# Two transformer blocks in one program: a scan's work moved between engines, the second mixer's closing stages merged with its projections, and the second experts' first nine weight pieces loaded one stage earlier

## The chip, the cores and the metric

The program runs on one core of one Trainium2 chip. The core has TensorE (PE, matrix products; its weight loads are a row of their own, PEld), VectorE (DVE), ScalarE (ACT), GpSimd (POOL) and SyncE (SP, which here only issues transfers), each with its own instruction stream, joined by semaphores. The metric is the device time of one execution in microseconds.

## The reference, cut to what matters

Two blocks run one after the other on 512 tokens of width 1024, all in float32. The first has a token mixer with neighbourhood attention and a two-way state-space scan (SSD), then 16 experts. The second has a mixer of two branches, then 32 small experts. Three places matter here.

The scan, chunk by chunk (128 tokens), for 4 groups of 8 heads and in both directions:

```python
    x = (xs * dt[..., None]).reshape(Bsz, nc, SSD_CHUNK, SSD_GROUPS, R, P)
    states = jnp.einsum('bclgn,bcgrl,bclgrp->bcgrpn', Bc, decay_to_end, x)
    def step(h, inp):
        dec, st = inp
        return dec[..., None, None] * h + st, h
    ...
    y_diag = jnp.einsum('bcgls,bcgrls,bcsgrp->bclgrp', cb, Lm, x)
    y_off = jnp.einsum('bclgn,bcgrpn,bcgrl->bclgrp', Cc, jnp.moveaxis(h_prev, 0, 1), jnp.exp(a_cs))
```

It runs first over the context (256 tokens, only the states count), then over the 512 tokens (states and y). The state after the last chunk of each direction is not used by anything.

The second mixer: `merged = gate_rw * (y_rw @ w_branch_rw) + gate_mla * (y_mla @ w_branch_mla)`. y_rw is a recurrent mix that ends in a normalisation by head, a scale and shift, a bonus and a gate. y_mla is an attention whose queries and keys come from a projection down (672 columns), two root-mean-square norms, a rotation by position, and projections up.

The second experts (`hier_moe`): each token goes to 2 of 32 experts, `(silu(gt) * up) @ w_down[e]`, with gt and up from a 1024x512 matrix of the expert.

## The kernel before, in words

Work is cut into stages. A stage is a function that holds one instruction stream for each engine (`@block.tensor`, `@block.vector` and so on), and between two stages all engines meet at a barrier. Inside a stream the order is the order of the code, and semaphores say who waits for whom.

`ssd_scan` walks 48 units (direction, chunk, group): 16 of the context, then 32 of the main tokens, of which the first 16 write y for the first time and the last 16 add to it. For each unit POOL makes `xd` and `xde` (inputs times step size, times decay) and, for main units, `seg_in` (L1277, 128x1024). PE makes the new state's part `st` (L1313), the product with the old state `yo` (L1318), the next unit's `seg` and `cb` (L1300, L1302, one PSUM buffer each) and `yd` (L1323). ACT takes exp of `seg` into `lx`. DVE masks `cb` into `cbm` (L1345), multiplies `lx` by it (L1349), decays the state (L1358), adds `st` (L1359), and makes y (L1362 to L1371). A helper `Steps` (its objects are called `link`) makes an engine wait for its own last result.

The second mixer ends in this chain of stages, all at barriers: `rw_states` (the recurrence), `rw_finish` (norm, scale, bonus and gate of y_rw, on DVE), a transposition of y (`rw_y_t`), the branch product (`rw_br`), the load of a block of constants, the projection down (`p_mla`), `mla_rows` (norms and rotation tables), two transpositions (`mla_qn_t`, `mla_kvn_t`), `mla_up`, and `causal_attention`. Weights for the next projection are asked for by SP while the last one runs (`WeightsAhead`, two buffers).

The second experts: `route_experts` (stage `hm_choose`) scores and ranks tokens. `fine_experts` (stage `hm`) then runs in a loop whose count is read from the device; in this trace it goes round once. It takes the experts in 16 pairs. For a pair, two 2 MB pieces (gate and up, `gu`) and one 2 MB piece (`down`) are needed. Three pieces are loaded in the choice stage (`hm_kept`), the other 45 go through a ring of five slots that SP starts to fill when `hm` begins:

```python
            for n in range(len(ring.order)):
                if n >= HM_SLOTS:
                    kind, u, _ = ring.order[n - HM_SLOTS]
                    sp.wait_ge({"gu": gu_done, "down": down_done}[kind], u + 1)
                ring.load(sp, n)
```

POOL gathers the tokens of each pair by index from DRAM (L3462, `xrow`), PE turns them (L3487), DVE scales them (L3582), PE multiplies by the weights (L3501), and so on.

## Time and profile before

| what | value |
|---|---|
| runs before | 3734.84, 3745.22, 3734.08 us, median 3734.84 us |
| the profiled execution | 3730.5 us, of which the span of the trace is 3728.7 us |
| PE busy | 3155.3 us, 85% of the span |
| DVE, ACT, POOL busy | 1146.8, 478.1, 320.3 us |
| mean granted TensorE clock | 0.925 of full speed |
| moved by DMA | 669.34 MB |

The profiled execution is one run, 4.3 us below the median of the three that were timed. Busy times are sums of instruction durations. The ends of matrix products are modelled, and a product can show as busy while the next one has started. A bracket behind a row gives the idle time of that engine before the row and, after the arrow, what ended it.

### The profile page before, as it was taken

How to read it: one execution, taken by the hardware profiler on the slowest of the kernel's cores; microseconds unless marked ns; L12 is line 12 of the kernel's file. 1: busy time of each engine (PE TensorE's matmuls, PEld its weight loads, DVE VectorE, ACT ScalarE, POOL GpSimd, SP SyncE). 2: the span in 40 equal slices, each digit the busy share in tenths (PEclk: the TensorE clock that was granted, in tenths of full speed). 3: DMA queues.
4: the chain of work that ended last, by engine and by line, in shares of the span. 5: the costliest groups of instructions: out<-in, count | busy, mean ns of one | idle time of the engine just before them, and what ended most of it. 6: DMA issues, size and time to landing. Idle time of an engine off the chain costs nothing. (4 is left out here: it accounts for less than half of the span.)

```text
span 3728.7 us, 38059 instructions
## 1 busy us (share of the span) xinstructions
PE 3155.3 (85%) x15800; PEld 1675.7 (45%) x15800; DVE 1146.8 (31%) x2119; ACT 478.1 (13%) x898; POOL 320.3 (9%) x261
## 2 busy tenths in 40 slices
PE   6997799996989999598999999987967577995974
PEld 4444545562654444444434443434447443534331
DVE  2234602554893200401011101113264613512112
ACT  1002500111112100100000000001123101301111
POOL 0003000003972000000000000000012100000000
PEclk9998998996999999699999999998989788995997
DMA  6621021100001221399999999995100120015996
GB/s 255 248 68 46 1 71 46 46 23 1 23 1 68 90 68 45 159 410 418 423 416 423 415 428 424 423 388 179 34 1 3 52 76 24 23 45 215 398 425 277
DMA packets 130497, 669.34 MB, mean 180 GB/s; under 512 B 15994, under 2 KB 44061, under 8 KB 97305
## 3 DMA queue, kind: packets, MB, share of 16 engines
q1 hardware_dynamic: 115385, 630.24, 42.1%
q10 hardware_dynamic: 11488, 28.31, 2.0%
q0 software_dynamic: 3456, 8.39, 0.6%
q8 instruction: 125, 2.05, 0.2%
q14 instruction: 43, 0.35, 0.0%
HBM read 653.28 MB, written 14.69 MB: 179 GB/s over the span
## 5 line engine op out<-in xcount | busy, mean ns | idle before, releaser
L1907 PE MATMUL ec_wide<-ec_ring,ec_xg 128*64 128x512 f32 x2048 | 457.9, 601 | 24.3 <-issue 18.6
L1907 PEld LDWEIGHTS ec_wide<-ec_ring,ec_xg 128*64 128x64 f32 x2048 | 148.2, 138 | 313.9 <-issue 309.7
L1941 PE MATMUL ec_acc<-ec_ring,ec_hidT 128*64 128x512 f32 x1024 | 232.8, 608 | 38.4 <-DMA ec_ring<-in_w_exp_down 36.3
L2066 DVE TENSOR_SCALAR ec_xg<-ec_piece,ordered 128x128 f32<-128x128 f32 x64 | 21.9, 404 | 583.0 <-PE ec_piece L1955 583.0
L1941 PEld LDWEIGHTS ec_acc<-ec_ring,ec_hidT 128*64 128x64 f32 x1024 | 84.5, 140 | 184.6 <-issue 184.6
L3501 PE MATMUL hm_gu<-hm_ring,hm_xg 128*64 128x512 f32 x480 | 110.8, 615 | 23.7 <-DMA hm_ring<-in_moe_w_gu 22.3
L1955 PE MATMUL ec_piece<-ec_sel,x 128*128 128x128 f32 x512 | 124.4, 405 | 3.3 <-DVE ec_sel L2048 3.3
L1955 PEld LDWEIGHTS ec_piece<-ec_sel,x 128*128 128x128 f32 x512 | 122.9, 336 | 9.1 <-issue 5.7
L2631 POOL TENSOR_TENSOR solve_T<-const_rw,solve_T 128x512 f32<-128x512 f32 x8 | 10.1, 1266 | 1330.2 <-DVE solve_T L2669 1330.2
L1107 PE MATMUL conv_main<-hT,conv_early 128*128 128x512 f32 x192 | 85.3, 599 | 1.6 <-DVE bcT L1183 1.6
L526 PE MATMUL p_rkv_acc<-ahead_rkv,h2mT 128*128 128x384 f32 x256 | 84.5, 494 | 2.3 <-DVEq L534 2.3
L1107 PE MATMUL conv_main<-hT,conv_late 128*128 128x512 f32 x192 | 85.8, 600 | 0.0
L2030 ACT ACTIVATE ec_hidT<-ec_acc 128x512 f32<-128x512 f32 x32 | 17.4, 594 | 519.3 <-PE ec_acc L1930 519.3
L3501 PEld LDWEIGHTS hm_gu<-hm_ring,hm_xg 128*64 128x64 f32 x480 | 39.2, 141 | 94.3 <-issue 92.5
L1277 POOL TENSOR_TENSOR ssd_seg_in<-const_all,a 128x1024 f32<-128x1024 f32 x32 | 77.3, 2416 | 0.6 <-PE ssd_cb L1302 0.6
L2081 DVE TENSOR_TENSOR branch<-branch,ec_piece 128x512 f32<-128x512 f32 x64 | 44.0, 687 | 107.2 <-PE ec_piece L1973 107.2
L1973 PE MATMUL ec_piece<-ec_y,ec_selT 128*128 128x512 f32 x128 | 63.8, 622 | 7.3 <-DVE ec_selT L2075 6.1
L1286 POOL TENSOR_TENSOR ssd_xde<-ssd_xd,dec 128x512 f32<-128x512 f32 x48 | 68.7, 1431 | 3.8
L1300 PE MATMUL ssd_seg<-ssd_seg_in,const_all 128*128 128x512 f32 x128 | 62.4, 610 | 4.7 <-DVE ssd_cbm L1345 4.7
L526 PEld LDWEIGHTS p_rkv_acc<-ahead_rkv,h2mT 128*128 128x128 f32 x256 | 49.4, 193 | 37.0 <-DVEq L534 2.5
L2676 DVE TENSOR_TENSOR solve_T<-solve_T,solve_wide 64x512 f32<-64x512 f32 (+1 forms) x80 | 50.5, 632 | 50.0 <-PE solve_wide L2562 42.0
L1358 DVE TENSOR_TENSOR ssd_state<-ssd_state,dec 128x512 f32<-128x512 f32 x40 | 59.7, 1492 | 18.4 <-PE ssd_st L1313 18.4
(620 smaller groups left out, 5016.5 us busy)
## 6 DMA issues: line engine op xcount, KB each, us to landing
ec_ring<-in_w_exp_gate SPq DMA_DIRECT2D x64, 2048.0 KB, 14.0
ec_ring<-in_w_exp_up SPq DMA_DIRECT2D x64, 2048.0 KB, 22.2
ec_ring<-in_w_exp_down SPq DMA_DIRECT2D x64, 2048.0 KB, 17.7
hm_ring<-in_moe_w_gu SPq DMA_DIRECT2D x30, 2048.0 KB, 18.8
hm_ring<-in_moe_w_down SPq DMA_DIRECT2D x15, 2048.0 KB, 15.9
ahead_qkv<-in_w_in SPq DMA_DIRECT2D x10, 2048.0 KB, 9.6
key<-in_w_ada ACTq DMA_DIRECT2D x4, 2048.0 KB
v<-in_w_ada ACTq DMA_DIRECT2D x4, 2048.0 KB, 10.2
```

The costliest lines, as they stand in the source:

```text
L526: last = pe.matmul(acc[0:rows, bank, 0:cols], stat(j), mov(j), start=(j == 0), stop=(j == kt - 1))
L1107: last = pe.matmul(main[:, i % 2, :], w[:, j, m * P:(m + 1) * P], hT[:, j, :], start=(j == 0), stop=(j == KD - 1))
L1277: pool.tensor_tensor(seg_in[:, m % 2], cum.unsqueeze(1).to_broadcast([P, HG, P]), spread(a[:, tile(u), hs:hs + HG], P), ALU.mult).then_inc ...
L1286: pool.tensor_tensor(xde[:, n % 2].rearrange("p (h e) -> p h e", h=HG), xd[:, n % 2].rearrange("p (h e) -> p h e", h=HG), spread(e2, 64), ...
L1300: pe.matmul(seg[:, h, :], k.const("after" if d == 0 else "before"), seg_in[:, m % 2, 4 * h:4 * h + 4].rearrange("p h l -> p (h l)"), start ...
L1358: link(dve.tensor_tensor(sv, sv, spread(e3, 64), ALU.mult))
L1907: last = pe.matmul(wide[half(e), b, :], xg[:, u % 2, j, half(e)], w[e][:, a, b * 512:(b + 1) * 512], start=(j == 0), stop=(j == KD - 1))
L1941: last = pe.matmul(acc[half(e), h, :], hidT[:, f, half(e)], w[e][:, r, h * 512:(h + 1) * 512], start=(f == 0), stop=(f == FT - 1))
L1955: last = pe.matmul(piece[:, m % 2, i * P:(i + 1) * P], x[:, t, HALF * h + i::KD], sel[:, t, :], start=(t == 0), stop=(t == LT - 1))
L1973: pe.matmul(piece[:, m % 2, :], selT[:, t * P:(t + 1) * P], y[:, h * 512:(h + 1) * 512], start=True, stop=True).then_inc(piece_done, 1)
L2676: dve.tensor_tensor(x, x, wide[s][half(c), c, first * 256:512], ALU.subtract).then_inc(T_done[s], 1)
L3501: last = pe.matmul(gu[half(e), u % 2, :], xg[:, u % 2, j, half(e)], w[e][:, j, :], start=(j == 0), stop=(j == KD - 1))
```

## The change

Three parts, in one edit.

**Scan.** `seg_in` is made by ACT (8 copies of 128x128 with a scale each) in place of one POOL instruction. The decay of the state goes from DVE to POOL. POOL prepares unit n+1 before it decays the state for unit n. The last 8 units make no `xde`, no `st` and no new state.

```diff
+            def decayed(n):
+                main, d, c, g = units[n]
+                if main:
+                    pool.wait_ge(off_ready, mains.index(n) + 1)
+                pool.wait_ge(state_done, n - chain + 1)
...
+                pool.tensor_tensor(sv, sv, spread(e3, 64), ALU.mult).then_inc(state_decayed, 1)
+
+            inputs(0)
+            for n in range(len(units)):
+                if n + 1 < len(units):
+                    inputs(n + 1)
+                if chain <= n < kept:
+                    decayed(n)
...
+            def segment_inputs(m):
+                main, d, c, g = units[mains[m]]
+                if m >= 2:
+                    act.wait_ge(seg_ready, m - 1)
+                cum = k.const("upto" if d == 0 else "from")
+                for h in range(HG):
+                    col = d * SSD_H + g * HG + h
+                    ins = act.activation(seg_in[:, m % 2, h, :], cum, ACT.Copy, scale=a[:, tile(units[mains[m]]), col:col + 1])
+                ins.then_inc(seg_built, 1)
...
-                    link(dve.tensor_tensor(sv, sv, spread(e3, 64), ALU.mult))
+                elif n < kept:
+                    dve.wait_ge(state_decayed, n - chain + 1)
                     dve.tensor_tensor(state[:, d, g, :], state[:, d, g, :], st[:, :], ALU.add).then_inc(state_done, 1)
```

POOL in `ssd_scan`, some main units of before:

```order
L1277 TENSOR_TENSOR ssd_seg_in<-const_all,a 128x1024
L1283 TENSOR_TENSOR ssd_xd<-xs,dt 128x512
L1286 TENSOR_TENSOR ssd_xde<-ssd_xd,dec 128x512
L1277 TENSOR_TENSOR ssd_seg_in<-const_all,a 128x1024
L1283 TENSOR_TENSOR ssd_xd<-xs,dt 128x512
L1286 TENSOR_TENSOR ssd_xde<-ssd_xd,dec 128x512
```

and of the changed kernel:

```order
L1297 TENSOR_TENSOR ssd_state<-ssd_state,dec 128x512
L1279 TENSOR_TENSOR ssd_xd<-xs,dt 128x512
L1286 TENSOR_TENSOR ssd_xde<-ssd_xd,dec 128x512
L1297 TENSOR_TENSOR ssd_state<-ssd_state,dec 128x512
L1279 TENSOR_TENSOR ssd_xd<-xs,dt 128x512
L1286 TENSOR_TENSOR ssd_xde<-ssd_xd,dec 128x512
```

The 128x1024 instruction is gone from POOL and a 128x512 one on the state stands in its place.

**Second mixer.** `rw_finish_and_down` runs the finish of y_rw on DVE and, in the same stage, the projection down on PE, with ACT copying its results. Its weights lie in a tile that is free by then (`T4`) and are loaded by SP during `rw_states`, as are the rows of the norm, the positions, the constants and the residual. `rw_branch_and_rows` holds the transposition of y, the branch product, the rows of the attention and the transpositions of its norms in one stage. The weights of the branch are loaded there, at its start, and with them those of `mla_up`. After `mla_up` and after the attention a clearing of semaphores with a barrier is added.

```diff
+        @block.tensor
+        def _(pe):
+            for i, (c, t) in enumerate(tiles):
+                if t == 0:
+                    pe.wait_ge(down_loaded[c], 16)
+                if i >= 4:
+                    pe.wait_ge(product_taken, i - 3)
+                for j in range(KD):
+                    last = pe.matmul(acc[:, i % 4, 0:width], hT[:, j, t * P:(t + 1) * P], down_w[:, c, j * width:(j + 1) * width], start=(j == 0), stop=(j == KD - 1))
+                last.then_inc(product_ready, 1)
...
         @block.sync
         def _(sp):
...
+            for b in range(2):
+                ahead.load_first(sp, b, k.dram["w_branch_rw_2"][0], NY, 512)
+            for (dst, src), up_loaded in up_moves:
+                sp.dma_start(dst, src).then_inc(up_loaded, 16)
+            for b in range(2):
+                sp.wait_ge(product_ready, 4 * (b + 1))
+                ahead.load_first(sp, b, *w_next)
...
+            for j in range(NY):
+                turn(j, lambda t: y[:, t, j * P:(j + 1) * P], P).then_inc(y_flipped, 1)
+            pe.wait_ge(y_taken, NY)
+            for m in range(3):
+                product(m)
             pe.wait_ge(table_ready, 2)
             for i in range(3):
...
+                turn(i, lambda t: table[:, i, t, :], MLA_QK).then_inc(flipped, 1)
+            product(3)
+            for i, (dst, scale, j) in enumerate(columns):
...
+                turn(3 + i, lambda t: source[:, t, j * P:(j + 1) * P], P).then_inc(flipped, 1)
+                if i in (1, 3):
+                    product(4 + i // 2)
+            product(6)
+            product(7)
```

PE from the end of the recurrence to `mla_up`, before (the number behind x counts products of one kind in a row; `rw_br_b` is the branch, `p_mla` the projection down):

```order
L2717 MATMUL states_out<-states_S,rw_GT 64x64 x56
L402 MATMUL rw_y_t_pt<-const_all,rw_y 128x128 x16
L526 MATMUL rw_br_b_acc<-rw_yT,ahead 128x512 x32
L526 MATMUL p_mla_acc<-ahead,h2mT 128x336 x64
L2902 MATMUL mla_rows_bank<-const_all,mla_rows_table 96x128 x12
L402 MATMUL mla_qn_t_pt<-const_all,mla_qn 128x128 x12
L402 MATMUL mla_kvn_t_pt<-const_all,mla_kvn 128x128 x8
L2946 MATMUL mla_up_pq<-mla_qnT,mla_up_wq 96x512 x3
```

and of the changed kernel (`rw_fin_acc` is the projection down, `mla_rows_acc` the branch, `mla_rows_flip` the transpositions):

```order
L2772 MATMUL states_out<-rw_K,rw_GT 64x64 x56
L2851 MATMUL rw_fin_acc<-rw_T,h2mT 128x336 x64
L3000 MATMUL mla_rows_flip<-const_all,rw_y 128x128 x16
L3010 MATMUL mla_rows_acc<-mla_o,ahead 128x512 x12
L3000 MATMUL mla_rows_flip<-const_all,mla_v 96x128 x12
L3010 MATMUL mla_rows_acc<-mla_o,ahead 128x512 x4
L3000 MATMUL mla_rows_flip<-const_all,mla_gate 128x128 x8
L3010 MATMUL mla_rows_acc<-mla_o,ahead 128x512 x4
L3000 MATMUL mla_rows_flip<-const_all,mla_gate 128x128 x8
L3010 MATMUL mla_rows_acc<-mla_o,ahead 128x512 x4
L3000 MATMUL mla_rows_flip<-const_all,mla_gate 128x128 x4
L3010 MATMUL mla_rows_acc<-mla_o,ahead 128x512 x8
```

The number of products is the same. The projection down now comes first, and the transpositions of the attention's rows stand between products of the branch.

**Second experts.** The ring has nine slots and holds all 48 pieces. Its first nine are loaded in the choice stage (three early, six behind the store of the normalised rows). Since a later round of the loop needs them again, POOL reloads them by index inside the loop. In the first round every index lies out of range, so that no row is fetched; PE still waits for these transfers' semaphores. DVE sets the indices (2 small instructions at the end of the choice and of each round).

```diff
-HM_SLOTS = 5
-HM_KEPT = (("gu", 0, 0), ("gu", 0, 1), ("down", 0, 0))
+HM_SLOTS = 9
...
+    def load_again(self, pool, n):
+        kind, u, e = self.order[n]
+        pool.wait_ge(self.first_loaded[n], 16)
...
+            pool.indirect_dma_start(place, None, rows, bass.IndirectOffsetOnAxis(ap=self.rows[:, expert:expert + 1], axis=0),
+                                    bounds_check=HM_E * P - 1, oob_is_err=False).then_inc(self.again[n], 16)
...
+        if n < HM_SLOTS:
+            pe.wait_ge(self.first_loaded[n], 16)
+            pe.wait_ge(self.again[n], 16 if job[0] == "gu" else 32)
...
+                if u in (1, 2):
+                    for n in range(5 * (u - 1), min(5 * u, HM_SLOTS)):
+                        ring.load_again(pool, n)
```

POOL in `hm`, before (DMA is an indexed transfer that POOL issues):

```order
L3456 MEMSET hm_xrow 128x2048
L3462 DMA hm_xrow<-hm_xn_rows,hm_index 128x1024 x16
L3469 DMA hm_ring<-hm_y_rows,hm_source 128x1024 x8
```

and of the changed kernel:

```order
L3591 MEMSET hm_xrow 128x2048
L3597 DMA hm_xrow<-hm_xn_rows,hm_index 128x1024 x2
L1874 DMA hm_ring<-in_moe_w_gu,hm_again_rows 128x4096 x4
L1874 DMA hm_ring<-in_moe_w_down,hm_again_rows 128x2048 x2
L3597 DMA hm_xrow<-hm_xn_rows,hm_index 128x1024
L1874 DMA hm_ring<-in_moe_w_gu,hm_again_rows 128x4096 x2
L1874 DMA hm_ring<-in_moe_w_down,hm_again_rows 128x2048 x2
L1874 DMA hm_ring<-in_moe_w_gu,hm_again_rows 128x4096
L3597 DMA hm_xrow<-hm_xn_rows,hm_index 128x1024 x13
L3607 DMA hm_ring<-hm_y_rows,hm_source 128x1024 x8
```

Eleven indexed transfers are new on POOL's queue: six behind the second gather of tokens, five behind the third.

## Rows read from the trace of the kernel before

**Rows 1.** Windows of five stretches: us, length, busy per engine, PEclk, DMA share, GB/s

```profile
877.00:940.00 63.00, 35.47 (x37) 9.57 (x38) 23.53 (x24) 1.28 (x1) 43.78 (x38) 0.50 0.10 34
940.00:1027.30 87.30, 87.30 (x420) 56.69 (x418) 77.07 (x95) 17.40 (x17) 80.49 (x46) 1.00 0.00 1
1027.30:1135.00 107.70, 91.74 (x412) 55.21 (x410) 102.39 (x113) 15.35 (x15) 70.54 (x45) 1.00 0.00 1
2957.00:3100.00 143.00, 75.79 (x240) 45.99 (x240) 50.48 (x78) 8.27 (x23) 8.54 (x12) 0.79 0.28 99
3449.00:3690.00 241.00, 200.17 (x952) 86.14 (x952) 34.21 (x68) 28.19 (x47) 12.85 (x13) 0.96 0.95 395
```

**Rows 2.** Timeline of the scan's context units: start us, us, engine, line

```profile
887.36 0.69 DVE L1354 COPY ssd_state<-ssd_st 128x512 f32<-128x512 f32 x1 [2.30 <-PE ssd_st L1313]
...
907.73 2.05 PE L1313 MATMUL ssd_st<-ssd_xde,bc_rows 128*128 128x512 f32 x2 [2.54 <-DVE ssd_state L1359]
...
912.32 2.04 PE L1313 MATMUL ssd_st<-ssd_xde,bc_rows 128*128 128x512 f32 x2 [2.54 <-DVE ssd_state L1359]
```

**Rows 3.** Timeline of one of the last 16 main units

```profile
1046.44 1.08 PE L1313 MATMUL ssd_st<-ssd_xde,b_rows 128*128 128x512 f32 x2
...
1046.75 1.04 POOL L1283 TENSOR_TENSOR ssd_xd<-xs,dt 128x512 f32<-128x512 f32 x1 [3.28 <-PE ssd_yd L1323]
...
1047.43 0.91 DVE L1371 TENSOR_TENSOR y<-y,ssd_off 128x512 f32<-128x512 f32 x1
1047.87 1.37 POOL L1286 TENSOR_TENSOR ssd_xde<-ssd_xd,dec 128x512 f32<-128x512 f32 x1
...
1048.57 1.75 DVE L1349 TENSOR_TENSOR ssd_lx<-ssd_lx,ssd_cbm 128x1024 f32<-128x1024 f32 x1
1048.69 1.95 PE L1300 MATMUL ssd_seg<-ssd_seg_in,const_all 128*128 128x512 f32 x4 [0.31 <-DVE ssd_cbm L1345]
...
1050.70 1.90 PE L1323 MATMUL ssd_yd<-ssd_xd,ssd_lx 128*128 128x64 f32 x16
```

**Rows 4.** Groups by line and form, ACT at 128x128: busy us, mean ns

```profile
L661 ACT ACTIVATE hT_tiled<-open_xf,mod,scales 128x128 f32<-128x128 f32 x8 | 3.7, 457 | 17.8 <-DVE hT L721 17.7
...
L3070 ACT ACTIVATE mla_pT<-mla_flip 128x128 f32<-128x128 f32 x8 | 2.0, 256 | 0.0
```

**Rows 5.** Timeline from the finish of y to the projections up

```profile
2959.05 2.29 DVE L2797 TENSOR_REDUCE rw_fin_mean<-rw_y 128x32 f32<-128x2048 f32 x1 [1.65 <-PEq L3247]
...
2981.11 2.29 DVE L2812 TENSOR_TENSOR rw_y<-rw_y,rw_g 128x2048 f32<-128x2048 f32 x1
...
2991.76 25.48 PE L526 MATMUL rw_br_b_acc<-rw_yT,ahead 128*128 128x512 f32 x59
...
3025.34 37.94 PE L526 MATMUL p_mla_acc<-ahead,h2mT 128*128 128x336 f32 x128 [8.10 <-DVEq L534]
...
3100.02 4.55 PE L2946 MATMUL mla_up_pq<-mla_qnT,mla_up_wq 128*96 128x512 f32 x6 [10.94 <-DMA mla_up_wkv<-in_mla_w_kv_up]
```

**Rows 6.** DMA issues: KB each, median us from issue to landing

```profile
ahead<-in_w_branch_rw SPq DMA_DIRECT2D x1, 1024.0 KB, 7.3
```

**Rows 7.** Timeline of stage hm, POOL and PE

```profile
3408.89 1.20 POOL L3462 DMA_INDIRECT hm_xrow<-hm_xn_rows,hm_index  x1 [2.14 <-DVE hm_index L3576]
...
3419.97 1.97 PE L3487 MATMUL hm_flip<-const_all,hm_xrow 128*128 128x128 f32 x8 [10.06 <-DMA hm_xrow<-hm_xn_rows,hm_index]
...
3423.26 9.33 PE L3501 MATMUL hm_gu<-hm_kept,hm_xg 128*64 128x512 f32 x32 [1.32 <-DVE hm_xg L3582]
...
3457.58 7.03 PE L3501 MATMUL hm_gu<-hm_ring,hm_xg 128*64 128x512 f32 x32
...
3502.14 7.09 PE L3501 MATMUL hm_gu<-hm_ring,hm_xg 128*64 128x512 f32 x32 [0.44 <-DMA hm_ring<-in_moe_w_gu]
...
3669.71 8.78 PE L3501 MATMUL hm_gu<-hm_ring,hm_xg 128*64 128x512 f32 x32 [4.31 <-DMA hm_ring<-in_moe_w_gu]
...
3694.55 0.95 POOL L3469 DMA_INDIRECT hm_ring<-hm_y_rows,hm_source  x1 [0.30 <-issue]
```

**Rows 8.** DMA issues, the third gather of tokens alone: us to landing

```profile
hm_xrow<-hm_xn_rows,hm_index POOLq DMA_INDIRECT x1, 3.9
```

321 lines of the change are left out of this document (192 added, 129 removed).

## The prediction, as it was put on record

> **What bounds the kernel now.** I read the windows first, since the busy share of the whole run mixes stages with different limits. In the scan's first stretch of 63 us TensorE is busy for only 35.47 us, at half clock; in the next, 16 main units, it is busy for all of 87.30 us, so PE is the limit there; in the last 16 it has 91.74 of 107.7 us and DVE has 102.39, so something other than PE sets the pace [rows 1]. The timeline says what: single units and the bracket in front of each product [rows 2, 3]. For the second mixer, the window 2957 to 3100 shows PE busy for half and DMA at 0.28: a chain of short stages, limited by waiting in turn [rows 1, 5]. For the second experts the window gives a DMA share of 0.95 at 395 GB/s with PE at 200 of 241 us: nearly balanced, DMA slightly in the lead [rows 1], which the brackets confirm, 0.44 us of wait at the sixth pair and 4.31 at the last [rows 7].
>
> **Scan.** Context units first. The first eight have no decay: period 0.69+2.30=2.99 us. The last eight take 912.32-907.73=4.59, with PE waiting 2.54 for DVE's addition [rows 2]. There DVE does decay and addition between two `st`. With the decay on POOL, DVE and PE are back at about 2.99, and POOL has `xd`, `xde` and the decay, three 128x512 operations at 1.04 alone [rows 3], with gaps about 3.3. So 8 x (4.59-3.3) = 10 us saved. The bounds: none if POOL's three are each 1.4 long, as `xde` beside DVE is (1.37, [rows 3]), which makes 4.4; 13 at 2.99.
>
> The first 16 main units are 87.3/16=5.46 us each with PE always busy [rows 1]; no edit removes PE work, so they stay. DVE (77.07/16=4.8) and POOL (80.49/16=5.0) lose work there. ACT gains 8 copies of 128x128 per unit: 17.40/16=1.1 [rows 1] plus 8 x 0.26 to 8 x 0.46 [rows 4] is 3.1 to 4.8, under 5.46; this edit is hidden by PE and costs nothing unless a copy takes over 0.54 us.
>
> The last 16 main units take 107.7/16=6.73. From `st` to `seg` there are 1048.69-1046.44=2.25 us, since `seg` waits for `cbm`, which stands on DVE behind the addition to y [rows 3]; that order stays. From `seg` to `yd` are 1050.70-1048.69=2.01, and `yd` takes up to 1.90 (its modelled end overlaps the next product, about 1.75 until then) [rows 3]. A closed cycle of 6.0 to 6.16 remains, above PE's 5.46; decay of the state, and POOL's long `seg_in`, which fill the rest to 6.73, are gone. 16 x (0.57 to 0.73) = 9 to 12; I take 11.5. The dropped work of the last 8 units changes little of it, since the cycle contains `st` only as a start, and PE's end is not the limit; at most its 1.08 x 8=8.6 us more.
>
> The two engines disturb each other: `y+=` takes 0.91 and ends at 1048.34, while `xd` ended at 1047.79; `xde` takes 1.37 against the 1.04 of `xd`; the multiplication of `lx` takes 1.75 and starts while `xde` runs [rows 3]. The Trainium skill, "SBUF — State Buffer", section "SBUF: two separate sides", says that DVE with two SBUF inputs and GpSimd share a port pair that is an exclusive lock for the whole instruction. Taken at its word it would speak against moving decay from DVE to POOL: it buys nothing in an operation that both are blocked by. Read so, the lock is held in a unit for three POOL operations and two to three of DVE, by the rows 3x1.04+1.75+0.91=5.8 at the most, just below the cycle of 6.0; the trace agrees that they lengthen each other, but not that it binds. Were it to bind in the first 16 too, that is the third rival below.
>
> Scan: -10-11.5, so **-22** (bounds -8 and -30).
>
> **Second mixer.** The recurrence ends on DVE at 2959.05-1.65=2957.40, and `mla_up` starts at 3100.02 [rows 5]: 142.6 us. The changed chain, from the same start: a gap of 1.65 as now, the projection down of 37.94 [rows 5], at 2959.05 to 2997.0. DVE's finish lies beside it: 2983.40-2959.05=24.35 [rows 5], 13.6 shorter, so free; if the copies of ACT held it up by a few us it would still be. Its weights are asked for a stage earlier (`T4`), in `rw_states`. One copy more (0.5) and a barrier (1.65) give 2999.1. Now the branch stage: its weights are only asked for at its start, 7.3 us to landing for one 1 MB piece [rows 6]; 16 transpositions of y and their copies lie under that. So products begin at 3006.4. 64 of them at 25.48/59 make 27.6 [rows 5]; 32 transpositions of 128 columns at a quarter of a product's 0.43 are 3.5 between them. 3037.5; a merge of one or two DVE operations 0.8, the next stage's gap 1.65 and the added clearing of semaphores about 1: `mla_up` at 3041. The wait of 10.94 for its weights [rows 5] is gone, since they are asked for with the branch's, some 40 us earlier. 3100.02-3041 = **-59**. What left: loading of constants between stages (3025.34-2991.76-27.6 is 6 us), the norms and turns after the projection, which ran alone (3100.02-3025.34-37.94=36.7 with the wait), and DVE's finish alone. The price of the load at the stage's start is the largest unknown: nothing if it lay under the turns entirely, 7.3 as taken, and twice that if y's two pieces and `mla_up`'s come one behind another (14.6). The norms run on DVE and ACT during the products; they lay within 36.7-10.94=25.8 before, at most 28 are there now, so 8 us more at most if a chain of them ends behind the products. Bounds: -45 and -64. A wait of over 7 us on PE may also start it at half clock, which I put in this same bound.
>
> **Second experts.** Gather by POOL at 3408.89; PE turned its rows at 3419.97, 11.1 us on, 10.06 of them waiting for DMA [rows 7], because SP's ring pieces fill the queues. Alone, a gather lands in 3.9 [rows 8]. After the change the ring is full before, so 3412.8, then 3423.26-3419.97=3.3 to the first `gu`: 3416.1. But PE now also waits for the empty transfers; these come behind the second gather on POOL: from 3411.9, two at about 1.25 (rows: 0.95 to 1.20), landing 3.9 more, 3418.3. I take 3417.5, -6. The third pair stood 34.3 us after the first (3457.58-3423.26) [rows 7], so 3451.8. Then the step per pair while weights were ahead is (3502.14-0.44-3457.58)/3=14.71 [rows 7]; 13 steps give 3643.0 for the last pair. Whether DMA allows that: before, ten pairs at DMA's pace took (3669.71-3502.14)/10=16.76, for three pieces 5.59 each [rows 7]. Refill starts when the first `gu` is done (3417.5+9.33=3426.8) and the last pair's needs 37 pieces more: 3426.8+206.8+5=3638.6, in balance with 3643, so PE is the limit now, barely. 3669.71-3643 = 26.7, less 0.8 for DVE's index instructions: **-26**. Bounds: -12 if the empty transfers' cost scales with rows and bytes (2 MB against 0.5 MB, 4 x 0.95=3.8 us each, the first pair waiting for two of them and the third behind nine) and PE's step is 15.8 by lost clock; -31 at a step of 14.1.
>
> The price of an empty indexed transfer is in no row; the nearest are the full gathers (0.95 to 1.20 us on POOL, 3.9 to landing, [rows 7, 8]), and an empty one may cost more on POOL, if making the list of rows is what takes time, or less. The Trainium skill, "DMA: Bandwidth & Descriptors", section "Anatomy of one DMA — SWDGE (gpsimd) path", gives 2.0 us plus bytes over 436 GB/s; for the 0.5 MB gather an estimate of 3.2, against the row's 3.9, and 2.0 for an empty one. By it the gate on the first pair would lie before 3416.1+1 and the term would be -27.
>
> **Sum.** -22-59-26 = -107. On the profiled execution, 3730.5 (span 3728.7 and 1.8 around it), 3623.5; that run is 4.3 below the median of 3734.84, on which the same sum gives 3627.8. I forecast 3626. A measurement of this kernel tells about 0.3%, 11 us, from no change.
>
> **Rivals.**
> 1. Experts: the indexed reloads or lost clock eat half of the third term (-12): 3640. For it: eleven new transfers on POOL, on PE's path. Against: only the first three pairs see them. 0.15.
> 2. Mixer: the branch stage pays for its loads in turn and its norms end last (-45): 3640. For it: 7.3 us in [rows 6] and 4 MB behind one another. Against: 28 us of products cover most. 0.1.
> 3. Scan: the state's chain now goes PE, DVE, POOL, and a state needed by `yo` arrives late; 24 units then go at 5.9 and not 5.46, +11, so -10 in all: 3638. For it: PE has no slack in [rows 1]; against: POOL makes the inputs of the next unit ahead of the decay, so only a decay of 1.04 stands in the chain. 0.1. This is what the lock would do if it bound; the rule is the one that I cite above from the Trainium skill, "SBUF — State Buffer".
> 4. Slower in all. Making a list of rows on POOL takes not 1 us but time in proportion to rows times bytes, at a rate that no row bounds. Before the third pair's gather stand nine pieces' worth; below 34.3+12 us (5 us each) it is hidden. Over that all of PE waits: at t us a piece the loss is 9t-46, which beats 107+11 from t=18. For it: no row of an indexed 2 MB transfer; against: the 0.95 to 1.20 of the 0.5 MB one. 0.03. No change within 11 us needs this same case at t between 17 and 19, or the lower bounds of all three parts (-8, -45, -12) with a new wait of 54 us; for both together 0.02.
>
> The forecast itself, 3610 to 3642 by its bounds, has 0.6. For 8 in 10 the range takes in rivals 1 to 3 together with small shortfalls: 3606 to 3660. Faster 0.95, same 0.02, slower 0.03.
>
> **What would show it.** Context period 3.3 us and not 4.59; first main units still 5.46, last 6.0; ACT's copies under 0.5. One block of products of 38 us from about 2959 with DVE's finish beside it, a wait of near 7 before the branch, `mla_up` near 3041 less the scan's gain. First `gu` 6 us earlier relative to its gather, step 14.7 to the end, no DMA bracket over 1 before the last pairs. I am wrong if the first 16 main units lengthen, if PE waits for POOL's indexed transfers in later pairs, or if PE's step in the ring grows past 15.5.

## The result, and the profile after

The changed kernel runs in 3633.11 us (median of 4, 3625.31 to 3636.84) against 3736.16 us for the kernel before (median of 4); the ratio is 0.9717, 95% interval 0.9694 to 0.974. That is 103 us less. The forecast was 3626, with 3606 to 3660 as its range, so the median lies 7 us above it. The profiled execution is the slowest of the four, 3636.84 us, and its span is 3634.9, so the two profiled executions are only 93.8 us apart. The rest of this section says where.

The windows of the changed kernel, for the first and the last 16 main units, the second mixer's middle and the second experts (columns as in [rows 1]):

```profile
937.40:1024.70 87.30, 87.30 (x419) 56.63 (x417) 56.76 (x79) 55.13 (x147) 62.56 (x46) 1.00 0.00 1
1024.70:1119.80 95.10, 82.97 (x397) 52.12 (x395) 66.04 (x88) 47.54 (x126) 39.90 (x30) 0.99 0.00 1
2947.50:3029.50 82.00, 73.26 (x240) 43.24 (x241) 42.58 (x66) 14.15 (x35) 4.05 (x5) 0.94 0.23 81
3375.00:3590.00 215.00, 190.57 (x931) 79.78 (x930) 33.15 (x65) 25.83 (x43) 12.85 (x13) 0.97 0.98 410
```

Against [rows 1]: the first 16 main units take the same 87.3 us with PE always busy, and DVE has fallen from 77.07 to 56.76 us and ACT risen from 17.40 to 55.13 in them. The last 16 take 95 and not 108. In the mixer PE does the same work in 82 us and not 143. In the experts DMA's share rose from 0.95 to 0.98.

The timeline of the changed kernel, context units 10 and 11 and one of the last 16 main units:

```profile
916.48 2.04 PE L1329 MATMUL ssd_st<-ssd_xde,bc_rows 128*128 128x512 f32 x2 [1.08 <-DVE ssd_state L1390]
919.61 2.04 PE L1329 MATMUL ssd_st<-ssd_xde,bc_rows 128*128 128x512 f32 x2 [1.09 <-DVE ssd_state L1390]
...
1030.26 1.10 PE L1329 MATMUL ssd_st<-ssd_xde,b_rows 128*128 128x512 f32 x2
...
1031.46 0.69 DVE L1402 TENSOR_TENSOR y<-y,ssd_off 128x512 f32<-128x512 f32 x1
1031.65 1.41 POOL L1286 TENSOR_TENSOR ssd_xde<-ssd_xd,dec 128x512 f32<-128x512 f32 x1
1032.39 1.75 DVE L1381 TENSOR_TENSOR ssd_lx<-ssd_lx,ssd_cbm 128x1024 f32<-128x1024 f32 x1
1032.51 1.95 PE L1315 MATMUL ssd_seg<-ssd_seg_in,const_all 128*128 128x512 f32 x4 [0.29 <-DVE ssd_cbm L1377]
1033.02 2.02 POOL L1297 TENSOR_TENSOR ssd_state<-ssd_state,dec 128x512 f32<-128x512 f32 x1
1034.52 1.90 PE L1341 MATMUL ssd_yd<-ssd_xd,ssd_lx 128*128 128x64 f32 x16
1035.64 2.43 ACT L1355 ACTIVATE ssd_seg_in<-const_all,a 128x128 f32<-128x128 f32 x8
1036.25 1.08 PE L1329 MATMUL ssd_st<-ssd_xde,b_rows 128*128 128x512 f32 x2
```

The context step is 919.61-916.48=3.13 us where it was 4.59 [rows 2], and the main step is 1036.25-1030.26=5.99 where units of 6.7 and 7.05 took turns before. `seg` still waits 0.29 us for `cbm`, as in [rows 3]. ACT's 8 copies take 2.43 us, 0.30 each.

PE in the mixer of the changed kernel, from the recurrence's end to the projections up:

```profile
2949.30 36.40 PE L2851 MATMUL rw_fin_acc<-rw_T,h2mT 128*128 128x336 f32 x128 [1.83 <-PEq L209]
2987.82 2.96 PE L3000 MATMUL mla_rows_flip<-const_all,rw_y 128*128 128x128 f32 x16 [2.12 <-PEq L3395]
2993.37 13.23 PE L3010 MATMUL mla_rows_acc<-mla_o,ahead 128*128 128x512 f32 x24 [2.60 <-DMA ahead<-in_w_branch_rw]
...
3029.51 4.48 PE L3070 MATMUL mla_up_pq<-mla_qnT,mla_wq 128*96 128x512 f32 x6 [2.23 <-PEq L209]
```

Only 2.60 us of waiting for a transfer is left, and nothing of the 10.94 of [rows 5]. DVE in the same stage:

```profile
2965.25 0.35 DVE L2874 RECIPROCAL rw_fin_var<-rw_fin_var 128x32 f32<-128x32 f32 x1 [4.55 <-ACT rw_fin_var L2861]
...
2975.52 2.29 DVE L2882 TENSOR_TENSOR rw_y<-rw_y,rw_g 128x2048 f32<-128x2048 f32 x1
```

The finish waits 4.55 us for the square root, which stands behind ACT's third copy, and still ends at 2977.8, 8 us ahead of PE.

The experts' stage of the changed kernel, POOL and PE:

```profile
3342.37 1.20 POOL L3597 DMA_INDIRECT hm_xrow<-hm_xn_rows,hm_index  x1 [2.14 <-DVE hm_index L3710]
...
3345.69 0.99 POOL L1874 DMA_INDIRECT hm_ring<-in_moe_w_gu,hm_again_rows  x1 [0.30 <-issue]
3346.98 1.97 PE L3625 MATMUL hm_flip<-const_all,hm_xrow 128*128 128x128 f32 x8 [3.59 <-DMA hm_xrow<-hm_xn_rows,hm_index]
...
3350.27 8.82 PE L3637 MATMUL hm_gu<-hm_ring,hm_xg 128*64 128x512 f32 x32 [1.32 <-DVE hm_xg L3716]
...
3379.86 7.04 PE L3637 MATMUL hm_gu<-hm_ring,hm_xg 128*64 128x512 f32 x32
...
3525.89 7.04 PE L3637 MATMUL hm_gu<-hm_ring,hm_xg 128*64 128x512 f32 x32
3543.20 7.09 PE L3637 MATMUL hm_gu<-hm_ring,hm_xg 128*64 128x512 f32 x32 [3.04 <-DMA hm_ring<-in_moe_w_gu]
3559.67 7.09 PE L3637 MATMUL hm_gu<-hm_ring,hm_xg 128*64 128x512 f32 x32 [2.17 <-DMA hm_ring<-in_moe_w_gu]
3575.95 8.62 PE L3637 MATMUL hm_gu<-hm_ring,hm_xg 128*64 128x512 f32 x32 [4.28 <-DMA hm_ring<-in_moe_w_gu]
```

The first gate product comes 7.9 us behind its gather's start, where it came 14.4 behind it [rows 7]. Between the third and the thirteenth pair a step is (3525.89-3379.86)/10=14.60 us, and no wait for DMA shows before the fourteenth.

To compare stages I took the first start of one tile's products and the first start (or last end) of the next one's from the timelines of all the kernels run. The kernels scan_only, mixer_only and ring_only have one part of the change each and are explained below. "List" in the last two lines is PE's first product for the list of tokens (`hm_list`), which stands ahead of the first gather. Lengths in us:

| stretch | before | changed | scan_only | mixer_only | ring_only |
|---|---|---|---|---|---|
| convolution to first state product | 290.1 | 295.7 | 290.1 | 290.5 | 290.1 |
| scan | 254.2 | 233.6 | 233.5 | 254.4 | 254.2 |
| first experts | 957.0 | 961.1 | 961.8 | 967.1 | 958.6 |
| recurrence's end to projections up | 143.4 | 82.0 | 146.1 | 81.7 | 143.8 |
| attention | 103.4 | 106.0 | 104.9 | 106.0 | 106.3 |
| experts: list to first gate product | 17.4 | 10.9 | 17.5 | 17.4 | 11.7 |
| experts: from there to the last product down | 265.5 | 244.6 | 261.0 | 260.3 | 246.5 |

Between the two profiled executions the three parts give -20.6, -61.4 and -27.4, together -109.4. The 15.6 us that the spans don't show stand in stretches that no edit touches (5.6 in the convolution, 4.1 in the first experts, 2.6 in the attention, the rest in small pieces). Over all the kernels run the convolution's stretch varies from 290.1 to 295.7 and the first experts' from 953.6 to 967.1, with no pattern by kernel. The mixer's stretch, too, varies with the mixer's code unchanged: 81.7 to 84.2 in the nine kernels that have the whole of its change, 143.4 to 146.1 in the three that have none of it. So a difference between two traces of up to some 2.5 us in the mixer, 5 us in the convolution or 13 us in the first experts says nothing about an edit.

### The profile page after: what moved, and what is told of

It reads as the page before. It is cut to its first block and busy times, and to the rows that moved or that the text cites. A ratio compares the mean times of both kernels' runs of the same rounds, so it can differ in the third digit from the quotient of the medians.

```text
span 3634.9 us, 38139 instructions
## 1 busy us (share of the span) xinstructions
PE 3149.1 (87%) x15784; PEld 1669.1 (46%) x15784; DVE 1072.0 (29%) x2063; ACT 558.7 (15%) x1166; POOL 283.7 (8%) x264
## 3 DMA queue, kind: packets, MB, share of 16 engines
q8 instruction: 124, 2.03, 0.2%
## 5 line engine op out<-in xcount | busy, mean ns | idle before, releaser
L2084 ACT ACTIVATE ec_hidT<-ec_acc 128x512 f32<-128x512 f32 x32 | 17.4, 594 | 523.1 <-PE ec_acc L1984 523.1
L1355 ACT ACTIVATE ssd_seg_in<-const_all,a 128x128 f32<-128x128 f32 x256 | 77.8, 389 | 1.8 <-PEq L1757 1.8
L3656 PE MATMUL hm_acc<-hm_ring,hm_hidT 128*64 128x512 f32 x256 | 63.6, 642 | 2.1 <-ACT hm_hidT L3688 1.6
L526 PE MATMUL na_br_g_acc<-hT,ahead_na 128*128 128x512 f32 x128 | 56.9, 607 | 7.7 <-ACTq L534 7.7
## 6 DMA issues: line engine op xcount, KB each, us to landing
hm_ring<-in_moe_w_down SPq DMA_DIRECT2D x16, 2048.0 KB, 28.5
```

Source lines behind the costliest of these rows:

```text
L526: last = pe.matmul(acc[0:rows, bank, 0:cols], stat(j), mov(j), start=(j == 0), stop=(j == kt - 1))
L1355: ins = act.activation(seg_in[:, m % 2, h, :], cum, ACT.Copy, scale=a[:, tile(units[mains[m]]), col:col + 1])
L3656: last = pe.matmul(acc[half(e), h, :], hidT[:, u % 2, f * P + e * SLOTS:f * P + (e + 1) * SLOTS], view[:, e * FT + f, h * 512:(h + 1) * 51 ...
```

## The experiments

All were timed beside the kernel before. Medians in us, ratio to before with its interval:

| kernel | median | ratio |
|---|---|---|
| scan_only | 3716.98 | 0.9944 (0.9926 to 0.9962) |
| mixer_only | 3677.51 | 0.9841 (0.9823 to 0.9858) |
| ring_only | 3714.34 | 0.9945 (0.9928 to 0.9963) |
| ring_no_again | 3636.76 | 0.9726 (0.9708 to 0.9743) |
| scan_decay_dve | 3642.59 | 0.9747 (0.9727 to 0.9767) |
| scan_seg_pool | 3672.25 | 0.9813 (0.9791 to 0.9836) |
| scan_mask_first | 3619.02 | 0.9677 (0.9658 to 0.9696) |
| mixer_finish_first | 3659.72 | 0.9786 (0.9767 to 0.9805) |
| ring_late | 3650.78 | 0.9780 (0.9763 to 0.9797) |
| ring_five_early | 3652.61 | 0.9789 (0.9768 to 0.9811) |
| mixer_up_late | 3645.84 | 0.9767 (0.9750 to 0.9785) |
| scan_mask_mixed | 3621.54 | 0.9693 (0.9671 to 0.9716) |

The first four had 3736.42 us of before beside them, the next four 3738.74, the last four 3735.83. Since an interval is 13 to 17 us wide, the stage lengths decide most of what follows, and the medians confirm them.

### The three parts one by one

scan_only, mixer_only and ring_only are the kernel before with one part of the diff each (the hunks of `ssd_scan`; those of the second mixer; those of the ring and its users).

> The kernel before with the scan's part of the change alone. Theory (the three parts are independent and add up): in the changed kernel's trace the scan, from its first state product to its last product, takes 20.6 us less than in the trace of before, so 3736 - 21 = 3715 us, and both experts' loops and the second mixer take what they took. Rival (the scan's gain is given back behind it, by a clock that is granted lower after a denser stretch): under 10 us less in all, 3726 or more, with a stage behind the scan longer than before.

Measured: 3716.98, scan 233.5. The rival's number falls, since the whole saved 19.4 us and not under 10. Its sign is there, though: the mixer's stretch is 146.1, the longest of the three kernels that have the old mixer (143.4 and 143.8 in the others). One trace can't tell that from chance, and it is 2.7 us at most.

> The kernel before with the second mixer's part alone. Theory (parts add up): from the recurrence's last product to the first of the projections up 61 us less (82 instead of 143.4), so 3736 - 61 = 3675 us. Rival (the mixer's gain is partly repaid in the attention, which in the changed kernel's trace ran 3.5 us longer than before): the attention is again 3 to 4 us longer and the whole is at 3679.

Measured: 3677.51, stretch 81.7. The attention was 106.0, but it was 104.9 and 106.3 in the two kernels without the mixer's part, and mixer_up_late (below), which has the change of the stages ahead of it, shows 103.4 again. So 103.4 and 106 both occur with either mixer, and the longer attention is no price of the change.

> The kernel before with the ring's part alone. Theory (parts add up): first gate product 6.5 us sooner after the stage's start, pairs at 14.1 us until the last three, stage shorter by 27 us: 3736 - 27 = 3709 us. Rival (the choice stage pays for the six pieces that now load beside it, by transfers that it waits for): the choice stage longer by 3 us or more and the whole above 3712.

Measured: 3714.34, 5 us short of the theory; but the choice stage was 42.7 us against 42.4, so the rival is not the reason. The gate product came 5.7 us sooner and the rest took 246.5. The missing 5 us are in the reference: scan_only and mixer_only have the ring of before, and took 261.0 and 260.3 us for what took 265.5 in the profiled execution of before. The first and the third gate product of mixer_only (those of the kernel before stand at 3423.26 and 3457.58 in [rows 7]):

```profile
3376.77 8.53 PE L3586 MATMUL hm_gu<-hm_kept,hm_xg 128*64 128x512 f32 x32 [1.32 <-DVE hm_xg L3667]
...
3405.92 7.04 PE L3586 MATMUL hm_gu<-hm_ring,hm_xg 128*64 128x512 f32 x32
```

From the first to the third pair the two kernels took 34.3 and 29.2 us for the same work. The windows over just these two pairs, before and mixer_only, show why:

```profile
3423.26:3457.58 34.32, 30.22 (x116) 12.55 (x117) 4.95 (x10) 1.15 (x3) 1.98 (x2) 0.73 0.54 216
3376.77:3405.92 29.15, 25.04 (x114) 10.30 (x116) 4.95 (x10) 1.15 (x3) 1.98 (x2) 0.89 0.58 230
```

The granted TensorE clock was 0.73 of full speed in one and 0.89 in the other, and the whole 5.2 us lie in PE's busy time. Leaving the profiled execution of before out for that reason, the ring is worth (17.4+260.6)-(11.3+245.5)=21 us, with the means of scan_only and mixer_only on one side and of the changed kernel and ring_only on the other, and ring_only's 22 us by medians agrees. The three medians alone save 19.4, 58.9 and 22.1, together 100.4, against 103.05 for the whole: the parts add up.

### The scan

```diff
-                if chain <= n < kept:
-                    decayed(n)
...
-                    dve.wait_ge(state_decayed, n - chain + 1)
+                    e3 = dec[:, t, 64 + g * HG:64 + (g + 1) * HG]
+                    sv = state[:, d, g, :].rearrange("p (h e) -> p h e", h=HG)
+                    link(dve.tensor_tensor(sv, sv, spread(e3, 64), ALU.mult))
```

> The changed kernel with the decay of the state back on DVE (seg_in stays on ACT, the last 8 units still make no state). Context units 8 to 15 go back from 3.13 to 4.59 us, +11.7, in any theory. For the last 16 main units, theory A (the decay on DVE is what filled the cycle from 6.0 to 6.73): the first 8 of them return to 6.7, +6, so the scan takes 233.6 + 17.7 = 251; the last 8, without decay, stay at 6.0. Theory B (POOL's long seg_in, which blocked DVE's operations, filled it): they stay at 6.0 and the scan takes 245. Whole kernel 3645 to 3651 us.

Measured: context step 4.58 again, the last 16 still 5.99, scan 243.0 us. Theory B. The decay on POOL buys only the context units (9.4 us); the cycle of the last 16 fell to 5.99 without it, which leaves `seg_in`'s move off POOL. Nor did the dropped work of the last 8 units bring it: their step is 5.93 in both kernels, against 5.99 in the 8 ahead of them.

```diff
+                if main:
+                    m = mains.index(n)
+                    if m >= 2:
+                        pool.wait_ge(seg_ready, m - 1)
+                    cum = k.const("upto" if d == 0 else "from")
+                    pool.tensor_tensor(seg_in[:, m % 2], cum.unsqueeze(1).to_broadcast([P, HG, P]), ...
...
-            segment_inputs(0)
-            segment_inputs(1)
```

> The changed kernel with seg_in back on POOL as one 128x1024 operation (the decay stays on POOL beside it). POOL then has 3 x 1.04 and 2.3 us alone, 5.4 us, more where DVE is in its way (1.4 and 2.0 for two of them in the changed kernel's trace), so 6.5 to 7. Theory A (POOL and DVE exclude each other and POOL would become the limit): first 16 main units at 6.5 to 7 and not 5.45, +17 to +25, all in the scan, 3650 to 3660. Theory B (the sides overlap and PE stays the limit): first 16 stay at 5.45, last 16 within 0.3 of 6.0, under +5 in all.

Measured: 3672.25, scan 266.1, which is 32.6 us more than in the changed kernel and 11.9 more than before. Steps in the first 16 went between 5.9 and 7.5 us. One of them in this kernel:

```profile
975.10 1.63 DVE L1384 TENSOR_TENSOR ssd_lx<-ssd_lx,ssd_cbm 128x1024 f32<-128x1024 f32 x1
975.72 1.90 POOL L1293 TENSOR_TENSOR ssd_xde<-ssd_xd,dec 128x512 f32<-128x512 f32 x1
977.59 1.04 POOL L1304 TENSOR_TENSOR ssd_state<-ssd_state,dec 128x512 f32<-128x512 f32 x1
978.76 0.69 DVE L1393 TENSOR_TENSOR ssd_state<-ssd_state,ssd_st 128x512 f32<-128x512 f32 x1 [2.03 <-POOL ssd_state L1304]
980.84 1.08 PE L1336 MATMUL ssd_st<-ssd_xde,b_rows 128*128 128x512 f32 x2
981.14 1.90 POOL L1284 TENSOR_TENSOR ssd_seg_in<-const_all,a 128x1024 f32<-128x1024 f32 x1 [2.52 <-issue]
```

`xde` takes 1.90 us where it takes 1.04 alone, because it starts inside DVE's multiplication of `lx`; DVE then stands 2.03 us for the decay. Theory A: the first 16 took 19.8 us more than in the changed kernel, within its 17 to 25. What it didn't price is the last 16, at some 6.8 us a unit and 12.8 us more in all. (POOL alone takes 1.90 us for `seg_in`, and not the 2.3 that I had put there.) So the two moves are one: the decay may go to POOL only because `seg_in` leaves it.

```diff
+            def mask(m):
+                dve.wait_ge(seg_ready, m + 1)
+                dve.tensor_tensor(cbm[:, m % 2, :], cb[:, 0:P], ...).then_inc(masked, 1)
...
+                    if m + 1 < len(mains):
+                        mask(m + 1)
                     dve.wait_ge(diag_ready, m + 1)
```

> The changed kernel with DVE masking cb of the next unit before it adds the finished unit to y. My reading of the last 16 units (seg waits for cbm, which stands behind the two additions to y on DVE, and that alone holds the cycle at 6.0): the cycle falls to PE's 5.45, 16 x 0.54 = 8.7 us less, scan 225, whole 3624 to 3625. Rival (DVE's own 5.0 us a unit with the waits for its last results are already the limit): the multiplication of lx then ends no earlier, yd starts as late as before, and the cycle stays at 5.9 to 6.0, under 2 us.

Measured: scan 225.4 as expected, but not as expected inside: the first 8 of the last 16 units stay at 5.95 (the rival's number), and the last 8, which make no state, fall to 4.86, below the 5.45 that I took for PE's limit. These units have no `st` (1.08 us as a row), so PE's own limit is lower there, and PE's rows follow one another without a wait. The whole is 3619.02 us. In the first 8 of this kernel:

```profile
1038.59 2.06 DVE L1386 TENSOR_TENSOR ssd_lx<-ssd_lx,ssd_cbm 128x1024 f32<-128x1024 f32 x1
1039.53 2.02 POOL L1297 TENSOR_TENSOR ssd_state<-ssd_state,dec 128x512 f32<-128x512 f32 x1
...
1041.68 0.69 DVE L1395 TENSOR_TENSOR ssd_state<-ssd_state,ssd_st 128x512 f32<-128x512 f32 x1 [1.03 <-POOL ssd_state L1297]
```

The decay takes 2.02 us and the addition waits 1.03 us for it; the next `st` waits for the addition. scan_mask_mixed tests that, with the decay of main units on DVE:

```diff
-                if chain <= n < kept:
+                if chain <= n < kept and not units[n][0]:
                     decayed(n)
```

> The changed kernel with cb masked first (as in scan_mask_first) and the decay on DVE for main units, on POOL for context units alone. In scan_mask_first the first eight of the last 16 units stayed at 5.95 us, with POOL's decay at 2.02 us beside DVE's multiplication of lx and DVE's addition 1.03 us behind it. Theory (that pair excludes each other and the decay's delay holds the cycle): with the decay on DVE itself these eight units fall to 5.45 to 5.6, the scan to 221 to 222 us, the whole to 3615. Rival (DVE is full: five operations of 0.7 and the one of lx leave no room for a sixth): 6.0 or more, scan 226 or more, 3620.

Measured: these units at 5.77, scan 223.6, whole 3621.54 (not distinct from scan_mask_first). Between theory and rival: the decay beside `lx` on POOL costs 0.18 us a unit. The other 0.3 above PE's 5.45 is DVE's list, as the rival has it: DVE's rows show no idle time in these units. But that list is long because POOL is beside it:

```profile
1040.76 2.06 DVE L1386 TENSOR_TENSOR ssd_lx<-ssd_lx,ssd_cbm 128x1024 f32<-128x1024 f32 x1
```

This multiplication starts 0.40 us behind the start of POOL's `xde` (1.37 us) and takes 2.06 us. In the last 8 units, which have no `xde`, it takes 1.21.

In both kernels the scan is shorter than in the changed kernel, by 8.2 and 10.0 us. The medians are 14 and 12 us lower; the intervals of their ratios overlap that of the changed kernel a little, so the stage lengths carry this.

### The mixer

```diff
+            pe.wait_ge(finished, 1)
             for i, (c, t) in enumerate(tiles):
```

(`finished` is set by DVE's last operation of the finish, and ACT takes the square root before its copies.)

> The changed kernel with PE waiting for DVE's last operation of y_rw's finish before it starts the projection down, so that the two lie one behind the other. Theory (what was overlapped is worth its whole length): the stretch from the recurrence's last product to the projections up grows by DVE's finish, 24.4 us in the trace of before, from 82 to 106, whole 3657; the rest of the mixer's gain, 61 - 24 = 37 us, is of the loads that moved ahead and the norms beside the branch. Rival (the finish beside the products runs slower than alone, by waits for ACT's square root or for POOL): it takes 28 us or more beside them and 24 alone, so that under 24 us are lost.

Measured: 3659.72, the stretch 109.0, +26.9 us and so 2.6 more than the finish, which is no more than the mixer's stretch varies. PE in this kernel:

```profile
2972.10 38.70 PE L2852 MATMUL rw_fin_acc<-rw_T,h2mT 128*128 128x336 f32 x128 [26.24 <-DVE rw_y L2882]
```

DVE's finish took 24.3 us (2947.70 to 2972.04), and the same 128 products took 38.70 where they took 36.40 in the changed kernel: the mean granted clock of the changed kernel's products was 1.00. Windows at their start in this kernel:

```profile
2972.00:2975.00 3.00, 2.90 (x5) 1.83 (x6) 0.04 (x1) 0.00 (x0) 0.00 (x0) 0.50 0.00 0
2975.00:2978.00 3.00, 3.00 (x9) 1.90 (x8) 0.00 (x0) 0.00 (x0) 0.00 (x0) 0.71 0.00 0
```

The first 3 us and part of the next 3 ran at 1.2 GHz (0.50), the rest at 2.4 GHz: that is the 2.3 us. But it isn't all a price of the 26.24 us of standing. In five of the kernels run these products took 38.09 us behind the same gap of 1.83 us that the changed kernel has, mixer_up_late (below) among them. Its row, and then the first 4 us in it and in the changed kernel:

```profile
2937.56 38.09 PE L2851 MATMUL rw_fin_acc<-rw_T,h2mT 128*128 128x336 f32 x128 [1.83 <-PEq L209]
```

```profile
2937.56:2941.56 4.00, 4.00 (x8) 2.45 (x9) 3.93 (x3) 0.00 (x0) 4.00 (x4) 0.57 0.02 4
2949.30:2953.30 4.00, 4.00 (x14) 2.74 (x15) 3.93 (x3) 0.00 (x0) 4.00 (x4) 1.00 0.02 4
```

So the clock at the start of this stage differs between kernels (0.57 or 1.00) with the stage's own code and gap the same, and is worth 1.7 us. What decides it was not tried. The rival falls: beside the products the finish took 28.5 us, yet nothing was lost by that.

```diff
-            for (dst, src), up_loaded in up_moves:
-                sp.dma_start(dst, src).then_inc(up_loaded, 16)
```

(moved from the branch stage to the start of `mla_up`.)

> The changed kernel with the weights of the projections up loaded at the start of their own stage, as before. Theory: the wait of 10.94 us of the kernel before [rows 5] comes back, less the 2.2 us that PE now waits there for the stage to begin, and PE then starts at a lower granted clock, which cost 2.3 us when it had stood for 26 us: 9 to 12 us, 3642 to 3645. Rival (the transfers that now run beside the branch slow its own weights, 2.60 us of wait): 2.6 us of it come back, 6 to 9 us.

Measured: 3645.84, the stretch 95.1, +13.1 us: the theory's sign, above its 9 to 12. In this kernel:

```profile
3030.86 4.18 PE L3073 MATMUL mla_up_pq<-mla_qnT,mla_wq 128*96 128x512 f32 x6 [13.44 <-DMA mla_wkv<-in_mla_w_kv_up]
```

The wait is 13.44 us in place of 2.23, which is 11.2 of the 13.1 us. Another 1.7 are the 38.09 us of the projection down shown above, in a stage that this edit doesn't touch. The clock cost nothing here: PE started the projections up at 0.50 in both kernels, and the row is 4.18 us long against 4.48. The branch's own weights didn't come sooner either (a wait of 2.97 against 2.60 us), so the rival falls. So of the mixer's 61 us, 24 to 27 are the finish beside the projection and 11 the weights of the projections up. The remaining 23 to 26, for constants, norms and transpositions beside the branch and for stages that fell away, were not tried one by one.

### The ring

```diff
-                if u in (1, 2):
-                    for n in range(5 * (u - 1), min(5 * u, HM_SLOTS)):
-                        ring.load_again(pool, n)
...
-            pe.wait_ge(self.again[n], 16 if job[0] == "gu" else 32)
```

> The changed kernel without the indexed reloads: POOL issues none of the eleven and PE waits for none; left out is what a second round of the loop would need, which this input does not have. Theory A (the empty transfers are hidden): same first gate product after the gather, same step of 14.1 us per pair, 0 to 1 us less, 3633. Theory B (they are on the path, as my 3417.5 instead of 3416.1 for the first gate product assumed, and their packets take time from the ring's transfers): the first gate product 1 to 2 us earlier, the last three pairs' waits for DMA (3.0, 2.2 and 4.3 us) smaller, 3 us or more less in all.

Measured: first gate product 10.9 us as with them, the rest 246.7 against 244.6, last waits 3.09, 2.16 and 4.31: theory A. Here the empty transfers cost nothing.

```diff
-            ring.load_first(sp, range(3, HM_SLOTS))
...
+            ring.load_first(sp, range(3, HM_SLOTS))
             for n in range(HM_SLOTS, len(ring.order)):
```

(from the choice stage to the start of the experts' stage.)

> The changed kernel with six of the nine first pieces (3 to 8) loaded when the experts' stage begins, as before, and not in the choice stage: nine slots, no early filling of them. Theory (the early start is what pays): the first gather again lands behind the pieces, first gate product at 17.4 us from the first list product and not 10.9; DMA then has to bring 43 pieces from about 3339 to the last pair's gate product, at 5.86 us a piece (the changed kernel's 216.8 us for 37) 252 us, to 3591 and not 3576, so the whole is 3633 + 14 = 3647. Rival (depth pays: nine slots let DMA run through, and what it brought early was only order): only the 6.5 us of the first pair are lost, 3639 to 3640.

Measured: 3650.78; first gate product at 25.6 us, and behind it 246.8, within the 244.0 to 248.4 of all kernels with nine slots. Neither account holds: nothing is lost later on, as the rival says, but the first pair loses 14.7 us and not 6.5. In this kernel:

```profile
3341.08 0.99 POOL L1874 DMA_INDIRECT hm_ring<-in_moe_w_gu,hm_again_rows  x1 [0.30 <-issue]
...
3347.00 1.97 PE L3625 MATMUL hm_flip<-const_all,hm_xrow 128*128 128x128 f32 x8 [8.22 <-DMA hm_xrow<-hm_xn_rows,hm_index]
...
3360.36 1.98 PE L3637 MATMUL hm_gu<-hm_ring,hm_xg 128*64 128x512 f32 x4 [11.39 <-DMA hm_ring<-in_moe_w_gu,hm_again_rows]
```

The gate product waits 11.39 us for empty transfers. Their median from issue to landing, for the first four `gu` ones, is 18.7 us in this kernel:

```profile
hm_ring<-in_moe_w_gu,hm_again_rows POOLq DMA_INDIRECT x4, 18.7
```

and in the changed kernel, where DMA's share is only 0.24 then (3345.69 to 3352.00) and not 1.01 as here (3341 to 3360):

```profile
hm_ring<-in_moe_w_gu,hm_again_rows POOLq DMA_INDIRECT x4, 2.1
```

```diff
-HM_SLOTS = 9
+HM_SLOTS = 5
```

> The changed kernel with five slots in place of nine, all five filled in the choice stage. Theory (early start pays, and depth only so far as it holds more of it): first gate product at 10.9 us as with nine, then 41 pieces at 5.86 us from the first refill (9 us behind the first gate product), 240 us, so the last pair's gate product 23 us later than with nine, 3656: nearly nothing is left of this part's gain. Rival (the ring of five was limited by slots that came free late, and so the gate product that comes 6.5 us sooner moves all behind it by 6.5): 3633 + 14 = 3647.

Measured: 3652.61; first gate product at 10.9, the rest 264.1, so 19.5 us more than with nine slots (theory 23, rival 14). The pairs wait for DMA from the fifth on. Its last one:

```profile
3591.04 9.47 PE L3637 MATMUL hm_gu<-hm_ring,hm_xg 128*64 128x512 f32 x32 [4.42 <-DMA hm_ring<-in_moe_w_gu]
```

Early filling with five slots leaves 3 us of gain (275.0 against 278 for the old ring), late filling with nine 5.5 us (272.4), both together 21. Early filling saves 6.5 us at the first pair by itself, and depth some 14 behind it; but depth has a price without early filling, since the reloads that it needs then land behind 12 MB. Late filling without the reloads was not tried, so what depth alone would give is not shown.

## Why the prediction was right, point by point

**The sum.** -107 was forecast for the profiled execution, which there is 3623.5. The median fell by 103, and the terms came out as -20.6 (forecast -22), -61.4 (-59) and, with the profiled execution of before left out for its clock, -21 (-26). The 5 us of the last term are most of the 7 us between forecast and median. Between the two profiled executions alone the terms look better than they are: there the experts show -27.4, and stretches that no edit touches gave back 15.6.

**Scan, context.** 3.3 us a unit forecast, 3.13 measured (10 us forecast; the context's stretch to the first main `st` fell by 9.7). The mechanism is right, the near-exact size partly luck: each step fell by 1.46 us and not 1.29, but it was seven steps and not eight, and the way from the last one to the first main `st` grew by 0.4.

**Scan, first 16.** Unchanged forecast, +0.25 us measured. ACT's copies, 2.43 us for eight with 1.02 for the exponential beside them, stay below PE. Right.

**Scan, last 16.** A cycle of 6.0 to 6.16 forecast, 5.99 measured; 11.5 us forecast, 11.2 measured (106.2 to 95.0, from `st` to the last `yd`). The size is right. That "decay of the state, and POOL's long `seg_in`" both fill the rest was wrong: scan_decay_dve shows it was `seg_in` alone. That `cbm` behind the additions to y held the cycle was right for the last 8 units, which fell from 5.93 to 4.86 with `cbm` first. For the 8 ahead of them it was half the story: they fell from 5.99 to 5.95 only, since there DVE's own list, stretched by POOL, stands right behind it (5.77 with POOL's decay gone).

**The rule of the port pair.** Ahead of the result I read it as speaking against a decay on POOL. In the rows shown here where POOL's operation starts inside DVE's multiplication of `lx` (at 1033.02, 975.72 and 1039.53 of three kernels), POOL takes 1.9 to 2.0 us in place of 1.04 and ends 0.9 behind `lx`, close to what a lock for a whole instruction would make it (the Trainium skill, "SBUF — State Buffer", section "SBUF: two separate sides"); the traces agree, near enough. In the changed kernel's scan all 23 of POOL's operations that start inside a multiplication of `lx` end 0.9 us behind it, and those that meet nothing of DVE's take 1.04. With `seg_in` gone from POOL this does not bind in the first 16 units. With `seg_in` left there POOL has 3x1.04+1.90=5.0 us a unit alone, under PE's 5.45, so its own work doesn't explain steps of 5.9 to 7.5; yet the scan is 11.9 us longer than before and 32.6 longer than in the changed kernel (scan_seg_pool). Rival 3 is real, on that condition.

**Mixer.** Projection 37.94 forecast, 36.40 measured. It is tempting to put that down to the gap ahead of it, 1.83 us and not 8.10 [rows 5], but five kernels with the gap of 1.83 took 38.09, so in this trace it is luck of the clock. Load at the stage's start: products forecast 7.3 us behind the start, measured 2993.37-2987.82=5.55, of which 2.60 were waiting. Products and transpositions 31.1 forecast, 33.9 measured. The difference is the clock that the forecast had put into its bounds only, here behind 2.60 us of waiting:

```profile
2993.37:3000.00 6.63, 6.63 (x9) 2.82 (x10) 1.48 (x8) 4.69 (x15) 0.00 (x0) 0.59 1.04 409
```

At 0.59 of full speed, 6.63 us lose 2.7. What closes the stage 3.45 forecast, 2.24 measured. The norms did end under the products. Every sign right, small errors that cancel. One reading was wrong without touching the sum: the 6 us for "loading of constants between stages" start from the row at 2991.76, which is the rest of a longer one cut by its window. The gap is the 8.10 in the bracket of [rows 5].

**Experts.** First gate product 5.8 us sooner forecast, 6.5 measured against [rows 7]. I let the empty transfers delay it by 1.4; ring_no_again shows 0. The step: 14.71 forecast, 14.60 measured. The term that was mis-sized is "the third pair stood 34.3 us after the first, so 3451.8": it took one execution's 15.6 and 18.8 us for the first two steps as a property of the kernel. Both other traces of the same ring have less (13.5 and 15.7 in mixer_only), as have those of nine slots (13.8 and 15.8 in the changed kernel, 15.6 and 15.8 in ring_only). So the last pair of before stood some 5 us late in that trace, by a granted clock of 0.73 as shown above, and the term should have been -21. DMA: 5.59 us a piece forecast, (3575.95-3359.13)/37=5.86 measured, with SP's first refill at 3359.13; the last three pairs waited 3.04, 2.17 and 4.28 us, so that "PE is the limit now, barely" holds only up to the thirteenth pair.

**Rivals.** Rival 1 did not occur (the reloads cost nothing here), but ring_late shows its mechanism, not by bytes and not by POOL's time: an empty transfer lands late when full ones were asked for ahead of it. Rival 2 did not occur. Rival 4 falls with the row of 0.99 us on POOL for an empty indexed transfer of 2 MB, against 18 us needed.

## What to carry to other kernels

Price a stage from more than one execution where the term is under 1% of the time, since one profile can hold 5 us of chance in a single stage, and look at the granted clock of the rows that a term rests on. Where two engines stretch each other's operations, as DVE and POOL do here, move an operation onto one of them only as another leaves it, and what was saved belongs to the pair. Deeper buffering and an earlier start are worth little each when the transfers are the limit and a full set of slots can only be had by starting early.
